# Row scaling behind the products of a second block, and its projection by seven products

## What is computed

```python
def rmsnorm_2(x, gain):
    y = xf * lax.rsqrt(jnp.mean(xf * xf, axis=-1, keepdims=True) + EPS)
    return y.astype(x.dtype) * gain

def second_block(...):
    for l in range(2):
        x = x + 0.5 * swiglu(rmsnorm_2(x, ffn1_norm[l]), ...)      # up_a, down_a
        x = x + token_mixing(rmsnorm_2(x, mix_norm[l]), ...)       # in, attention, out2
        x = x + 0.5 * swiglu(rmsnorm_2(x, ffn2_norm[l]), ...)      # up_b, down_b
    return rmsnorm_2(x, final_norm)
```

## Time and profile before

| | us |
|---|---|
| median of 3 runs | 3632.84 (3632.1 to 3633.59) |
| the profiled execution | 3630.63 |
| its span, first to last instruction | 3628.9 |
| TensorE busy | 3359.2 |
| VectorE busy | 1579.4 |
| ScalarE busy | 467.6 |
| mean granted TensorE clock | 0.959 of full speed |

### The profile page before, as it was taken

How to read it: one execution, slowest core, us unless ns; L and a number is a source line. 1 busy time by engine, 2 the same in 40 slices (tenths; PEclk the granted TensorE clock), 3 DMA queues, 4 the chain that set the end, 5 groups by cost and what they waited for, 6 DMA issues and landing times.

```text
span 3628.9 us, 32722 instructions
## 1 busy us (share of the span) xinstructions
PE 3359.2 (93%) x13204; PEld 2390.3 (66%) x13204; DVE 1579.4 (44%) x2682; ACT 467.6 (13%) x946; POOL 86.4 (2%) x102
## 2 busy tenths in 40 slices
PE   5999996689997999999889999989999998999997
PEld 2344443268886888854444888878887444478886
DVE  3125214456434655331463555345543216455543
ACT  1110101000001000000551000000000035300000
POOL 0000000000000000000200000000000120000000
PEclk9989997899998999999999999999999999999998
DMA  4214330012221222222201222222222230012221
GB/s 197 80 47 144 130 132 12 25 68 93 82 93 58 82 84 88 85 70 78 87 1 47 93 82 90 85 71 93 83 86 87 70 118 1 24 70 93 82 84 56
DMA packets 41831, 285.45 MB, mean 79 GB/s; under 512 B 5104, under 2 KB 5104, under 8 KB 10704
## 3 DMA queue, kind: packets, MB, share of 16 engines
q1 hardware_dynamic: 37584, 268.71, 20.9%
q0 software_dynamic: 4096, 14.64, 1.2%
HBM read 279.14 MB, written 2.10 MB: 77 GB/s over the span
## 4 chain that ended last, share of the span: by engine, by line
PE 89%; DVE 6%; ACT 2%; issue 1%; DVEq 1%; DMA 1%; POOL 0%; ACTq 0%; POOLq 0%
PE ps L730 55%; PE ps L389 20%; PE ps L408 5%; PE ps L868 2%; PE ps L900 1%; PE ps L882 1%; ACT arena L1128 1%; PE ps L674 1%; DVE ssq L443 1%; PE ps L661 1%; DVE arena L1686 0%; PE ps L684 0%; DMA h<-in_x 0%; PE ps L907 0%; DVE arena L1187 0%
## 5 line engine op out<-in xcount | busy, mean ns | idle before, releaser
L730 PE MATMUL ps<-arena 128*128 128x256 f32 x3584 | 825.8, 379 | 0.0
L730 PEld LDWEIGHTS ps<-arena 128*128 128x128 f32 x3584 | 681.0, 190 | 92.6
L389 PE MATMUL ps<-xn,ring 128*128 128x512 f32 x1472 | 640.9, 597 | 3.3 <-DVE xn L482 3.3
L730 PE MATMUL ps<-arena,ring 128*128 128x256 f32 x2272 | 525.6, 379 | 0.0
L389 PEld LDWEIGHTS ps<-xn,ring 128*128 128x128 f32 x1472 | 280.9, 192 | 358.3 <-issue 355.9
L730 PEld LDWEIGHTS ps<-arena,ring 128*128 128x128 f32 x2272 | 431.7, 190 | 58.7
L730 PE MATMUL ps<-xn,ring 128*128 128x256 f32 x1664 | 387.6, 387 | 13.4 <-ACT xn L1024 6.9
L730 PE MATMUL ps<-xn,arena 128*128 128x256 f32 x1664 | 393.1, 379 | 0.0
L730 PEld LDWEIGHTS ps<-xn,ring 128*128 128x128 f32 x1664 | 323.6, 195 | 67.2 <-issue 12.7
L730 PEld LDWEIGHTS ps<-xn,arena 128*128 128x128 f32 x1664 | 316.2, 190 | 43.0
L1447 DVE TENSOR_TENSOR arena<-arena,ps 128x512 f32<-128x512 f32 x124 | 85.1, 687 | 595.4 <-PE ps L730 595.4
(11 more groups left out here) (234 smaller groups left out, 2196.0 us busy)
## 6 DMA issues: line engine op xcount, KB each, us to landing
ring<-in_w_up_a SPq DMA_DIRECT2D x44, 1024.0 KB, 4.7
ring<-in_w_up_b SPq DMA_DIRECT2D x44, 1024.0 KB, 4.8
ring<-in_w_ff SPq DMA_DIRECT2D x32, 1024.0 KB, 4.7
ring<-in_w_ada SPq DMA_DIRECT2D x24, 1024.0 KB, 6.8
ring<-in_w_down_a SPq DMA_DIRECT2D x16, 1024.0 KB, 4.8
ring<-in_w_down_b SPq DMA_DIRECT2D x16, 1024.0 KB, 4.7
ring<-in_w_in SPq DMA_DIRECT2D x14, 1024.0 KB, 4.8
ring<-in_w_out SPq DMA_DIRECT2D x12, 1024.0 KB, 4.9
```

The costliest lines, as they stand in the source:

```text
L389: mm = nc.tensor.matmul(bank_ap(name, u), w, moving(k), start=(k == 0), stop=(k == K - 1))
L730: mm = nc.tensor.matmul(out_ap, w, operand(product, quad), start=at not in opened, stop=last_chunk and i == len(quads) - 1, skip_group_che ...
```

## The change

- In the second block, ScalarE writes `xn` = h times the norm's weight (`gained`) as soon as h is made, and products start on it. VectorE makes the operands' sums for one quad at a time (`quad_sums`), and the first pair of a stage goes quad by quad.
- The sum of squares over the features is one matmul with a matrix of ones ahead of a later pair (`row_sums`). VectorE makes the inverse from it (`row`, a reciprocal over 128x512), ScalarE the root, and `rs` holds the factor of each position on all partitions.
- Every pair of up tiles is multiplied by `rs` (two operations), ahead of Silu; the tiles of `in` are multiplied where they are copied; the values by columns of the factor (`r_col`).
- `in` runs as seven pairs through `seven`. The norms of c_q and c_kv and the rotated key part hang on pairs 3, 4 and 5; `in_v` waits until the last pair is taken.
- At the end of the first block the factor of `final1` and of the next norm come from two sums of squares (`both_rows`), and h is scaled later, in `tables`.
- Down stages and `out2` make tiles p and p + 4 together, the rotation of queries has places of its own in `TILES_2`, `mixed` lies in the arena, the load of the positions and GpSimd's clears wait for `xg`.

```diff
-TILES_2 = [("in", 14), ("in_v", 4), ("uq", 6), ("uk", 4), ("uv", 4), ("out2", 8)]
+TILES_2 = [("in_v", 4), ("uq", 4), ("turn", 1), ("uq", 2), ("turn", 1), ("uk", 4), ("uv", 4), ("out2", 8)]
...
-            def seven(name, layer, pair, groups, operand):
+            def seven(name, layer, pair, groups, operand, ready=None, order="aebdgcf", by_quads=False, ahead=None):
                 number, chunk_number = SEVEN_AT[name, layer, pair], SEVEN_CHUNK_AT[name, layer, pair * len(groups)]
                 bank0 = 4 * (number % 2)
                 homes = {"a": (3, 0), "e": (0, 0), "b": (0, 1), "g": (1, 0), "d": (1, 1), "c": (2, 0), "f": (2, 1)}
-                order = "aefcdbg" if pair == 0 else "aebdgcf"
                 opened = set()
                 wait(pe, "pair_taken", number - 1)
+                read = ahead(bank0) if ahead is not None else {}
...
+                    if by_quads:
+                        places = [(product, i) for i in range(len(quads)) for product in order]
...
+                        if ready is not None:
+                            pe.wait_ge(*ready(product, quads[i]))
+                        if at in read:
+                            pe.wait_ge(*read.pop(at))
...
+            def row_sums(*names):
+                def put(bank0, read):
+                    for name, layer, at, source in names:
+                        e = ROW_AT[name, layer]
+                        pe.wait_ge(sem("sq_added"), SQUARES[name if name != "s1" else "a", layer] + at)
+                        nc.tensor.matmul(row_bank_ap(name, layer), ones, source, start=True, stop=True)\
+                            .then_inc(sem("row_sum"), 1)
+                        read[row_bank(name, layer) - bank0] = (sem("row_read"), e + 1)
+                    return read
+                return lambda bank0: put(bank0, {})
...
+            def operand_ready(idx):
+                def ready(product, quad):
                     if product in "aef":
...
+                        return sem("xg"), DT * idx + 2 * quad + (1 if product == "a" else 2)
+                    return sem("xg_sums"), 4 * (idx - 1) + quad + 1
+                return ready
...
+                    elif p == 0:
+                        seven(name, layer, p, UP_QUADS, up_operand, operand_ready(idx), "aefdcbg", by_quads=True)
+                    elif p == 1 and idx == 0:
...
+                    elif p == 1:
+                        seven(name, layer, p, UP_QUADS, up_operand, None, "ebdgcaf",
+                              ahead=row_sums((tag, layer, DT, ssq[:, :])))
...
+                def turn_keys(bank0):
+                    pe.wait_ge(sem("projected"), 14 * layer + PE_IN + 1)
+                    nc.tensor.matmul(ps[:, bank0 + 3, :], swap, proj[:, PE_IN, :], start=True, stop=True)\
+                        .then_inc(sem("swapped"), 1)
+                    return {3: (sem("roped"), layer + 1)}
...
+                for p in range(IN_PAIRS):
+                    if p == 0:
+                        seven("in", layer, p, UP_QUADS, up_operand, operand_ready(3 * layer + 1), "aefdcbg", by_quads=True)
+                    elif p in (1, 3, 4, 5):
+                        ahead = {1: row_sums(("m", layer, DT, ssq[:, :])), 3: row_sums(("q", layer, 3, ssq[:, :])),
+                                 4: row_sums(("kv", layer, 2, ssq[:, :])), 5: turn_keys}[p]
+                        seven("in", layer, p, UP_QUADS, up_operand, None, "ebdgcaf", ahead=ahead)
+                    else:
+                        seven("in", layer, p, UP_QUADS, up_operand)
+                pe.wait_ge(sem("pair_taken"), SEVEN_AT["in", layer, IN_PAIRS - 1] + 1)
...
+                wait_evacuated(pe, "out2", DT - 1, layer=layer)
+                ffn("b", 3 * layer + 2, layer)
...
+            def gained(tiles, gain):
+                for u in tiles:
+                    nc.scalar.activation(xn[:, u, :], h[:, u, :], ACT.Copy, scale=gain(u)).then_inc(sem("xg"), 1)
...
+            def root(name, layer, dst):
+                act.wait_ge(sem("row_recip"), ROW_AT[name, layer] + 1)
+                nc.scalar.activation(dst, dst, ACT.Sqrt).then_inc(sem("row_root"), 1)
...
+                    act.wait_ge(sem("gate_scaled"), at * F_TILES + p + 1)
...
+                    act.wait_ge(sem("h_made"), DT * (at + 1) + 2 * p + 2)
+                    if gain is not None:
+                        gained((p, p + 4), gain)
+                    base = SQUARES[("m", layer) if tag == "a" else ("a", layer + 1)]
+                    for i, u in enumerate((p, p + 4)):
+                        act_square(act, base + 2 * p + i, square_of[:, i, :], h[:, u, :])
...
+                if last:
+                    b11, b12, b21, b22 = (xn[:, r:r + 4, half:half + HALF] for r in (0, 4) for half in (0, HALF))
+                    t1, t3, t2, t4 = (xn_t[:, n, :, :] for n in range(4))
+                    dve.wait_ge(sem("xg"), DT)
+                    for dst, x, y in ((t1, b12, b11), (t3, b22, b12), (t2, b22, t1), (t4, b21, t2)):
+                        nc.vector.tensor_tensor(dst, x, y, ALU.subtract).then_inc(sem("xg0_sums"), 1)
+                        dve.drain()
+                    next_sums(c + len(FF_QUADS) + 1)
...
+            def row(name, dst, width):
+                layer = now[0]
+                e = ROW_AT[name, layer]
+                dve.wait_ge(sem("row_sum"), e + 1)
+                nc.vector.tensor_scalar(dst, ps[:, row_bank(name, layer), :], 1.0 / width, EPS, ALU.mult, ALU.add)\
+                    .then_inc(sem("row_read"), 1)
+                nc.vector.memset(ssq[:, :], 0.0)
+                dve.drain()
...
+                nc.vector.reciprocal(dst, dst).then_inc(sem("row_recip"), 1)
+                dve.drain()
...
+            def quad_sums(idx, q):
+                b11, b12, b21, b22 = (xn[:, r, half:half + HALF] for r in (q, q + 4) for half in (0, HALF))
+                t1, t3, t2, t4 = (xn_t[:, n, q, :] for n in range(4))
+                dve.wait_ge(sem("xg"), DT * idx + 2 * q + 2)
+                nc.vector.tensor_tensor(t1, b12, b11, ALU.subtract)
+                nc.vector.tensor_tensor(t3, b22, b12, ALU.subtract)
+                dve.drain()
+                nc.vector.tensor_tensor(t2, b22, t1, ALU.subtract)
+                dve.drain()
+                nc.vector.tensor_tensor(t4, b21, t2, ALU.subtract).then_inc(sem("xg_sums"), 1)
...
+                    take_pair_of_tiles(SEVEN_AT["up_" + tag, layer, p])
+                    if p == 0:
+                        next_sums(chunk0 + 2)
+                        dve.wait_ge(sem("row_root"), ROW_AT[tag, layer] + (at > 0))
+                    dve.drain()
+                    nc.vector.tensor_tensor(first_tile(), first_tile(), rs[:, :], ALU.mult).then_inc(sem("gate_scaled"), 1)
+                    nc.vector.tensor_tensor(up_w[:, 0, :], up_w[:, 0, :], rs[:, :], ALU.mult)
+                    if p:
+                        next_sums(chunk0 + p + 2)
+                    else:
+                        dve.drain()
                     dve.wait_ge(sem("gated"), at * F_TILES + p + 1)
                     f = F_ORDER[p]
-                    nc.vector.scalar_tensor_tensor(hid2[:, f, :], gate_w[:, 0:2, :].rearrange("p o s -> p (o s)"), 0.5,
-                                                   up_w[:, 0, :], ALU.mult, ALU.mult)
+                    nc.vector.scalar_tensor_tensor(hid2[:, f, :], first_tile(), 0.5, up_w[:, 0, :], ALU.mult, ALU.mult)
...
+                    nc.vector.tensor_tensor(h[:, p, :], h[:, p, :], first_tile(), ALU.add).then_inc(sem("h_made"), 1)
+                    nc.vector.tensor_tensor(h[:, p + 4, :], h[:, p + 4, :], up_w[:, 0, :], ALU.add).then_inc(sem("h_made"), 1)
+                    if follows:
+                        quad_sums(idx, p)
+                        if last:
+                            next_sums(down0 + 3 * p + 4)
+                    base = SQUARES[("m", layer) if tag == "a" else ("a", layer + 1)]
+                    for i in range(2):
+                        dve_add_square(dve, base + 2 * p + i, square_of[:, i, :])
...
+                for p in range(IN_PAIRS):
+                    number = SEVEN_AT["in", layer, p]
+                    if p == 0:
+                        row("m", rs[:, :], D)
+                    elif p == 5:
+                        rope(proj[:, PE_IN, :], 3 * layer + 1, 4 * (number % 2) + 3, square_of[:, 0, :])\
+                            .then_inc(sem("roped"), 1)
+                    take_pair_of_tiles(number)
+                    if p + 2 < IN_PAIRS:
+                        next_sums(SEVEN_CHUNK_AT["in", layer, p + 2])
+                    if p == 0:
+                        wait_root("m")
+                        for st in range(ST):
+                            at = nc.vector.tensor_tensor_reduce(rq[:, 0:P], rs[:, st * P:(st + 1) * P], ident, 1.0, 0.0,
+                                                                ALU.mult, ALU.add, r_col[:, st:st + 1])
+                            dve.drain()
```

(30 more changed lines are left out.)

493 lines of the change are left out of this document (245 added, 248 removed).

## The result

The changed kernel takes 3539.33 us, median of 4 runs (3536.34 to 3543.19), beside 3632.85 of the kernel before, measured with it: a ratio of 0.9743, 95% interval 0.9726 to 0.976, so 93.5 us less. The forecast was 3526 with a range of 3513 to 3546: the sign and the range held, and of the 106.2 us promised 12.7 did not come. The profiled execution is the longest of the four, 3543.19 (span 3541.2). Against it the sum made from the profiled execution before (3630.63 - 106.2 = 3524.4) is 18.8 us short.

A forecast was written before the change was run, and what follows sets the result against it. TensorE, busy 93% of the span, was taken to bound the kernel. 106.1 us of norm losses, less 6.2, 3.4 and 0.9 kept, plus 2 x 5.3 from the projection, gave 106.2 us less: 3526.6 us, range 3513 to 3546.

The forecast's parts named there:

- the six places: Where a norm stands between two products in the second block and around it; together they lose 106.1 us.
- places 2, 4 and 5: down_a to `in`, down_b to layer 1's up_a, layer 1's down_a to `in`: losing 14.9, 16.95, 14.6 us; no stall kept.
- Place 3: out2 to up_b: loses 12.4 us, keeps 1.7 us, from 0.8 us of read and a row sum of 0.86.
- Edit 1: Norm leaves the path: products start on h times the weight, row factor multiplied in behind; place 1 keeps 6.2 us.
- place 1: ff2 to up_a, two norms in a row: loses 35.0 us, keeps 6.2 us, including a 3.55 us tile wait.
- Edit 2: Row scaling in 88 up pairs: VectorE 9.3 us a pair beside TensorE's 12.08, so cost 0.
- The rival on the slower side: Up pairs become VectorE's; decided at 13.3 us a pair; at 14 us the kernel takes 3696; chance 0.03.
- Edit 3: Projection as seven pairs: first product to `in_v` 95.3 us instead of 100.6, 5.3 us less per layer.
- GpSimd's clears: Four 1.80 us clears moved beside the sums of place 2: 0 to 7.2 us per layer, taken at 0.
- Rival 3: Projection's VectorE chain 5% to 10% longer, `in` 100 to 106 us per layer; 3536 to 3550 us; chance 0.17.
- main case: Whole kernel at 3515 to 3537 us, ends set by the projection's chain and place 1's clock plus lateness; chance 0.62.
- rivals 2 and 3: The former: clears or squares late at places 2 and 5, 2 to 7 us each; 3530 to 3545; chance 0.14.

The follow-up runs named there:

- The split experiment: Also "place 1 split": after, with up_a's first pair in layer 0 running three products on three tiles before asking for the fourth; 3538.42 us, ratio 0.9738.
- after: The changed kernel with the whole change, against the kernel before: 3539.33 us, ratio 0.9743; run again unchanged, 3539.22 us, ratio 0.9741.
- the two loads tried: After, with six or twelve more VectorE operations of 256 columns in each of 88 up pairs: 3546.67 us and 3757.28 us.
- values in other banks: After, with `in_v` writing to the four banks that pair 6 doesn't use, so it waits for pair 5 alone; 3528.78 us, ratio 0.9715.
- gap filled: After, with three matmuls that nobody reads in the idle 2.64 us ahead of `in_v` in each layer; 3535.79 us, ratio 0.973.
- squares first: After, with the squares of c_kv made ahead of the root of c_q in the projection's pair 2; 3535.33 us, ratio 0.9733.
- shifted: After, with two unread matmuls of 0.86 us each added to pair 10 of up_a in layer 0; 3541.59 us, ratio 0.9746.
- order by product: After, with the first pair of places 2 to 6 ordered by product instead of by quads, tile waits kept; 3554.95 us, ratio 0.9784.

## Why the forecast was right, and where it was off

**What bounds the kernel, the six places.** Right. The column sums' waits fell by 38.3 us, and the first products follow without idle time at places 2, 4 and 5.'s reading, that a place costs its whole length less the warm products and not only its waits, is what makes 106 us of 38. Place 3's forecast of 1.7 us was 1.6 to 1.7: 0.8 of wait on h and one sum of 0.86.

**Edit 1, what is late next.** Right at five places. VectorE's last addition of squares at place 2 ends 0.7 us ahead of the sum at 1565.88, where the working had 0.6. The order by quads carries it: without it 15.7 us come back. At place 1 the wait was 3.66 for 3.55 forecast. **The step that failed there** is the value taken for the clock: bounded by 0 and 3.1, taken at 0 "as products run on both sides"; it was 2.9 (6.76 us for 3.9), almost the other end, and "first products of up_a in layer 0 at half clock", which the prediction named as a sign of being wrong, is what the trace shows. The 0.85 us for the late row sum did not come, because TensorE, slowed by the half clock, arrived later. The split experiment shows the same account from its other side: 3.9 us of waits, wherever they stand.

**Edit 2, 88 pairs at nothing.** Right. Two rows of VectorE in after, and the stretch that answers to the earlier trace rows's last:

```profile
1421.04 0.69 DVE L1539 TENSOR_TENSOR arena<-arena,ps 128x512 f32<-128x512 f32 x1 [4.25 <-PE ps L766]
...
1429.88 0.43 DVE L1764 TENSOR_TENSOR arena<-arena 128x256 f32<-128x256 f32 x1
```

```profile
1967.00:2330.00 363.00, 363.00 (x1684) 319.55 (x1683) 204.64 (x347) 26.44 (x55) 0.00 (x0) 1.00 0.25 86
```

From 1421.04 to 1430.31 it is 9.3 us, the figure of the working, and TensorE is busy for all 363 us at full clock, beside a VectorE busy 0.56 of the time for 0.47 before. The rival on the slower side is a real one, and its threshold of 13.3 us lies between the two loads tried: at a mean of 11.4 us it costs 7.5, at 14.3 it costs 218 and turns the change into a loss.

**Edit 3, the projection.** Right in each stall to 0.8 us: squares of c_kv 1.35 for 1.6, keys 1.95 and 1.6 for 2.3, values 2.64 for 2.7; the 0.5 of the row's read was covered by the stall ahead of it, and showed as 1.1 once that was removed. What the term lacked was half clock behind the keys' stall: the 16 records after it take 5.25 us (1630.34 to 1635.59) for 3.45 (layer 1, behind 1.6 us, has none). It made layer 0 96.7 us; layer 1 came in at 94.65. Rival 3 (100 to 106 us per layer) did not happen.

**GpSimd's clears.** Taken at 0 of 0 to 14 us, and 0 it was. In order of time, GpSimd's first clear and VectorE beside it:

```profile
1559.36 1.80 POOL L592 MEMSET arena<- 32x2048 f32 x1 [406.31 <-ACT xn L1106]
```

```profile
1559.66 0.42 DVE L1665 TENSOR_TENSOR arena<-xn 128x256 f32<-128x256 f32 x1
...
1562.36 0.69 DVE L1519 TENSOR_TENSOR arena<-arena,ring 128x512 f32<-128x512 f32 x1
```

Both sides have the lengths that they have alone (1.80; 0.41 and 0.68). The row on the addition, 0.68 to 2.43, was the wrong neighbour. The Trainium skill's page "SBUF — State Buffer", section "Who interferes with whom", says that a VectorE instruction with two SBUF inputs contends with a GpSimd instruction that reads SBUF, not with one that only writes it. This trace agrees, in the case that the trace before could not show.

**The time.** It came 2.3 us above the main case's own 3515 to 3537, in the band that rivals 2 and 3 had for themselves, but by neither of their mechanisms: no sum of squares came late, and the projection did what it says. That the range held is in part luck: its upper end was put there for two events that did not happen. The forecast treated each stall as costing its own length once. A stretch at half clock behind a stall (place 1, the keys) and 4.8 and 6.4 us in an attention whose work is unchanged had no term. The working had the material: the earlier trace rows shows 16 records in 6.52 us behind a place's idle time, and a stall of 2.7 us was put directly ahead of a stage whose clock in the trace of before already was at 0.83 in parts.

**What stays open.** Why the attention of one kernel takes 226 and of another 231 us, and the same in both profiles of after. The idle gap ahead of it has a part in it (its removal is worth 10.4 us with the new banks, of which 5.3 are its length). The moment at which the stage runs, against the moments at which the granted clock changes, is a rival that no run here rules out, since the one that was to shift the stage did not. What separates the kernels that keep the gap (226.0 to 231.2) was not found. Nor was the way in which a gap acts 150 us later.

## What to carry to other kernels

A wait for a norm can be taken off the path when its factor is by row or by column of the product, and what then decides is the order of the next stage's first pair: use first what is ready first. In this kernel a TensorE stall of 2 to 4 us cost between its length alone and about twice that (3.66 + 2.9 at place 1, 1.95 + 1.8 or + 0 at the keys, 10.4 for 2 x 2.64 ahead of the values), behind it and in the next stage that has idle times of its own. So give such a stall a range, not its length, and remove small stalls ahead of a stage with idle times of its own first. Before an order of products is changed to hide a stall, look up which engine made it late: where TensorE comes earlier to the same chain, the wait only moves.

## What the runs showed of the hardware

- Idle times of 3.5 to 3.7 us (the tiles) were followed by 16 to 18 records at or near 1.2 GHz each time, at a cost of 1.8 to 2.9 us. Shorter ones were at some times and not at others: behind 1.95 us (the keys, layer 0) in five profiles (after twice, values in other banks, place 1 split, gap filled), at 1.8 us, and not in three (squares first, shifted, order by product); behind 2.64 us ahead of the values in 9 of 18 cases. Behind 1.6 us (the keys, layer 1) and 1.35 us (c_kv's squares) none was seen.
- A kernel's stretches at half clock repeat: 229.2 and 230.8 us of attention in both profiles of after and in its padded form, where the stage began at the same distance, to 0.1 us, though after's nine executions spread over 7.9 us (3536.3 to 3544.2). The kernel before spreads over 6.2 in 30 (3630.3 to 3636.5).
- Work of no use on TensorE can be free: three matmuls, 2.64 us, in an idle gap left the time the same or better (3535.8 us for 3539.2).
